# Fourteen projections of a decoder block as seven block products instead of eight, with GpSimd combining weights and VectorE summing blocks

## The chip, the cores and the metric

The program runs on one core of a Trainium2 chip. Its metric is the device time of one execution in microseconds. All of its data is f32. The core has TensorE (matmuls; PE in the profile, PEld its weight loads), VectorE (DVE), ScalarE (ACT), GpSimd (POOL) and SyncE (SP, which here only issues transfers). TensorE writes into eight banks of PSUM, of 128 partitions x 512 f32 each; the other operands are in SBUF.

## The reference, cut to what matters

The reference is one decoder layer on a sequence of 256 tokens of width 1024: a normalised input `h`, one wide projection of it split among a pooling mixer, an RWKV-7 mixer and a sparse attention (NSA), their merge, an output projection, and a mixture of experts.

```python
h = rms_norm(x, norm_mix)                     # 256 x 1024
t = h @ w_in                                  # all input projections at once
# columns: pooling 512 | r, k, v 3*512, loras 160 | q 1024, six K/V of 256, gates 48
pool_mixer: windows 2/4/8/16 over the sequence, pooled minus self, a map per group
rwkv7_mixer: u + (u_prev - u) * mu; decay, rates a, kk = k*k_k normalised; recurrent state
nsa_mixer: compressed keys kc, vc -> MLP; selected keys ks, vs; window keys kw, vw; 16 queries
x = x + merge(gated branches) @ w_out
x = x + hier_moe(rms_norm(x))
```

The change concerns 14 of the products `h @ w_in`, each with 256 of its columns.

## The kernel before, in words

All weights are repacked in chunks of 1 MB. A front chunk holds 256 columns of a 1024-deep matrix: 8 blocks `k` of 128 rows (on the partitions) by 256 columns. 48 front chunks pass through four slots of `ring` in the order of their numbers; SyncE loads chunk n once the chunk four before it has been given up (`taken`). Six steps of `ring` behind these four slots are not used for weights in the front: `bias`, `amat`, `qT` and `kT` lie there later. The 96 chunks of the experts follow, in the same way, in 23 slots all over SBUF.

`hT` is h transposed, 8 blocks of 128 channels by 256 tokens. A projection (`project`, L609 through `mm`) gives a chunk's 256 columns as two halves `m` of 128 rows, each the sum over 8 blocks `k` of a matmul with 128x128 weights and 256 tokens. That is 16 matmuls of 256 columns into one bank. In the order of the program `project` makes `pool1`, `rkv1` to `rkv6`, `kc`, `vc`, `q0` to `q3`, `ks` and `kw`. Other work stands in between: `wup` and `aup` (L698, L705: loras with 32 rows of weights), `kk0` and `kk1` (L714), the compression MLP (`mlp`, in two halves), `poolmix` (L729), `hidT`, `kcb`, `vcb`, `bonus` (L764), the scores `cs0` and `cs1` (L1007) and the transposes `tok` (L938).

ScalarE copies a bank that is full to SBUF (L1418) and frees it. VectorE then works on it: the pooling windows (`sums`), the mixing of each token with the one before it (`shift`: a subtract of 128x512 and two multiply-adds of 128x256 for each `rkv`), the squares for `kk`, the 16 scans of the decay (L1885), the windows of the compression, a reciprocal of 128x1024 (L1902) and a chain of twelve operations of 128x1024 to `rwkv_ready`. `raw` has two buffers, given back by `raw_used`. `tt`, `ts` and `stt` are VectorE's helpers, so that their lines (L1776, L1779, L1780, L1783) are those of many operations.

GpSimd clears three tiles, takes two roots for the normalisation (L1393), and has nothing more until 163 us (L1407, the masks of a triangular inverse, `lmask`).

The order of each engine is the order of the code. Every wait is on a semaphore; `bank_full` and `bank_free` of each bank count its uses in the order of `plan`. SyncE sends the relative bias through HBM (L546, L549) before it goes on with chunk 4.

## Time and profile before

| | us |
|---|---|
| median of 3 runs (lowest, highest) | 664.6 (664.16, 665.4) |
| the profiled execution | 663.38 |
| its span, first to last instruction | 661.6 |
| PE busy | 613.7 (93%) |
| DVE, ACT, POOL busy | 216.3, 141.3, 20.1 |

### The profile page before, as it was taken

The numbers are of one execution on the slowest core, as the hardware profiler recorded it, in microseconds if no ns is written. First come the engines' busy times: TensorE is split into PE (matmuls) and PEld (weight loads), VectorE is DVE, ScalarE is ACT, GpSimd is POOL, SyncE is SP. The second block draws the span as 40 slices with busy tenths as digits, with TensorE's granted clock in tenths as the row PEclk, the third lists the DMA queues.
The fourth block names the chain that finished last, engine by engine and source line by source line (L and its number), as shares of the span: only waits on it lengthen the run. The fifth ranks groups of instructions, "written<-read, shape, count | busy, mean of one in ns | idle before, by whom it ended". The sixth has DMA issues, their size and how long they took to land.

```text
span 661.6 us, 11832 instructions
## 1 busy us (share of the span) xinstructions
PE 613.7 (93%) x4992; PEld 450.1 (68%) x4992; DVE 216.3 (33%) x596; ACT 141.3 (21%) x356; POOL 20.1 (3%) x23
## 2 busy tenths in 40 slices
PE   8999999999999999999999999998999888858684
PEld 8988887888877777877778888886344433413241
DVE  3162548424333565345620122226111212012022
ACT  3010243132224263443531000001201111010013
POOL 1000000000200003000000000000000000000000
PEclk9999999989999999999999999999999999969698
DMA  8484335631211111011136996697999999999993
GB/s 326 185 314 181 127 128 190 259 124 65 85 46 65 66 64 65 12 55 66 64 115 276 423 419 229 255 423 274 398 421 419 421 421 420 420 423 421 421 394 129
DMA packets 27288, 158.96 MB, mean 240 GB/s; under 512 B 2896, under 2 KB 7136, under 8 KB 9440
## 3 DMA queue, kind: packets, MB, share of 16 engines
q1 hardware_dynamic: 24224, 137.71, 53.0%
q10 hardware_dynamic: 3008, 20.45, 7.4%
q8 instruction: 42, 0.69, 0.4%
q14 instruction: 14, 0.11, 0.0%
HBM read 157.07 MB, written 1.07 MB: 239 GB/s over the span
## 4 chain that ended last, share of the span: by engine, by line
PE 67%; issue 31%; ACT 1%; POOL 0%; DVE 0%; POOLq 0%; ACTq 0%; DVEq 0%
PE bank L609 45%; PE bank L840 5%; PE bank L938 3%; PE bank L641 2%; PE bank L967 2%; PE bank L987 2%; PE bank L624 1%; PE bank L997 1%; PE bank L951 1%; PE bank L1057 1%; PE bank L872 1%; PE bank L902 1%; PE bank L1007 1%; PE bank L891 1%; PE bank L1135 0%
## 5 line engine op out<-in xcount | busy, mean ns | idle before, releaser
L609 PE MATMUL bank<-hT,ring 128*128 128x256 f32 x864 | 199.9, 383 | 0.2 <-issue 0.2
L609 PEld LDWEIGHTS bank<-hT,ring 128*128 128x128 f32 x864 | 159.3, 190 | 31.4 <-issue 11.8
L609 PE MATMUL bank<-yT,ring 128*128 128x256 f32 x256 | 55.4, 379 | 0.0
L609 PEld LDWEIGHTS bank<-yT,ring 128*128 128x128 f32 x256 | 48.6, 190 | 6.6
L1418 ACT ACTIVATE work<-bank 128x512 f32<-128x512 f32 (+1 forms) x42 | 21.5, 511 | 110.9 <-PE bank L1239 48.9
L1776 DVE TENSOR_TENSOR work<-bank,table 128x512 f32<-128x512 f32 (+1 forms) x22 | 11.6, 544 | 94.1 <-PE bank L1232 85.5
L1285 PE MATMUL bank<-ring,work 128*32 128x512 f32 (+1 forms) x192 | 32.7, 615 | 10.4 <-DMA yT<-experts 7.2
L1232 PEld LDWEIGHTS bank<-work,tok 128*128 128x128 f32 x256 | 30.2, 192 | 10.0 <-issue 10.0
L1223 PE MATMUL bank<-ring,work 128*32 128x512 f32 x240 | 30.4, 612 | 2.6 <-DMA ring<-experts 2.6
L1232 PE MATMUL bank<-work,tok 128*128 128x128 f32 x256 | 31.5, 278 | 0.8 <-DVE work L1780 0.8
L1577 ACT ACTIVATE tok<-tok,small 128x128 f32<-128x128 f32 (+1 forms) x64 | 28.4, 445 | 14.5 <-DVE small L1995 12.6
L1293 PE MATMUL bank<-work 128*128 128x512 f32 (+1 forms) x68 | 29.9, 581 | 0.5 <-DVE work L2342 0.5
L609 PE MATMUL bank<-ring,work 128*128 128x256 f32 (+1 forms) x144 | 29.0, 358 | 0.0
L1783 DVE SCALAR_TENSOR_TENSOR work<-ring,bank 128x512 f32<-128x512 f32 x12 | 8.2, 687 | 58.7 <-PE bank L609 58.7
L609 PEld LDWEIGHTS bank<-ring,work 128*128 128x128 f32 x144 | 24.9, 190 | 2.8
L1293 PEld LDWEIGHTS bank<-work 128*128 128x128 f32 x68 | 12.2, 189 | 18.4 <-issue 17.3
L1783 DVE SCALAR_TENSOR_TENSOR work<-work,bank 128x256 f32<-128x256 f32 x8 | 3.4, 420 | 63.5 <-ACT work L1706 63.5
L1418 ACT ACTIVATE hT<-bank,table 128x128 f32<-128x128 f32 x12 | 3.6, 367 | 92.4 <-PE bank L1127 86.1
L1285 PEld LDWEIGHTS bank<-ring,work 128*32 128x32 f32 x192 | 8.6, 119 | 20.0 <-issue 17.9
L1995 DVE CUSTOM_DVE_ANT_0 tok<-bank,ring 128x128 f32<-128x128 f32 (+1 forms) x64 | 19.6, 352 | 7.5 <-PE bank L967 7.3
L1593 ACT ACTIVATE ring<-bank,small 128x256 f32<-128x256 f32 x24 | 10.1, 471 | 49.9 <-PE bank L609 49.9
L1418 ACT ACTIVATE t<-bank 128x512 f32<-128x512 f32 x16 | 9.6, 597 | 44.6 <-PE bank L840 26.6
(254 smaller groups left out, 748.3 us busy)
## 6 DMA issues: line engine op xcount, KB each, us to landing
ring<-front SPq DMA_DIRECT2D x47, 1024.0 KB, 4.9
ring<-experts SPq DMA_DIRECT2D x40, 1024.0 KB, 24.4
work<-experts SPq DMA_DIRECT2D x9, 1024.0 KB, 27.6
ring<-experts ACTq DMA_DIRECT2D x8, 1024.0 KB, 13.6
table<-experts SPq DMA_DIRECT2D x6, 1024.0 KB, 27.3
yT<-experts SPq DMA_DIRECT2D x6, 1024.0 KB, 26.8
hT<-experts SPq DMA_DIRECT2D x4, 1024.0 KB, 24.0
work<-experts ACTq DMA_DIRECT2D x3, 1024.0 KB, 27.8
```

The lines of the kernel that those rows point to most:

```text
L609: return first(pe.matmul(o, l, r, start=(k == 0), stop=(k == n - 1)))
L641: return first(pe.matmul(o[0:cols, col + i * P:col + (i + 1) * P], w[:, k, lo:lo + cols], hT[:, k, i * P:(i + 1) * P], start=(k == lo == i ...
L840: last = pe.matmul(o[rows, h * CH:(h + 1) * CH], left[rows, h, :], right[rows, h, :], start=True, stop=True)
L938: last = pe.transpose(o[:, b * P:(b + 1) * P], part, ident)
L967: last = pe.matmul(obank[p][:, hp * S:(hp + 1) * S], qT[rows, 2 * g + hp, i * P:(i + 1) * P], keys, start=True, stop=True)
L1223: last = pe.matmul(bank[4][CAP * e:CAP * (e + 1), :], gath[:, k, CAP * e:CAP * (e + 1)], w[:, e, :], start=(k == 0), stop=(k == KD - 1))
L1232: last = pe.matmul(o, tok[:, i, k * P:(k + 1) * P], sel[:, i, :], start=(i == 0), stop=(i == 1))
L1285: last = pe.matmul(o[CAP * e:CAP * (e + 1), 0:w], ghidT[:, f, CAP * e:CAP * (e + 1)], down[e][:, f, lo:lo + w], start=(f == 0), stop=(f == 1))
L1293: return pe.matmul(total[i][lo // 512][:, lo % 512:lo % 512 + w], wselT[:, i, :], ydown[:, lo:lo + w], start=False, stop=(gang == NGANG - ...
L1418: return act.activation(o, i_, ACT.Copy, scale=scale)
L1577: ins = act.activation(pb, pb, ACT.Exp, scale=-1.0, bias=astat[:, 8 * (n % 2) + b:8 * (n % 2) + b + 1], accum_out=astat[:, 16 + 8 * (n % 2 ...
L1995: ins = dve.tensor_tensor_reduce(prob[:, n % 2, bs], b0[:, bs], back, 1.0, FAR, ALU.add, ALU.min, astat[:, 8 * (n % 2) + b:8 * (n % 2) + b ...
```

## The change

A product of two 2x2 block matrices takes eight block products, or seven with 15 sums of blocks (Strassen's form as Winograd gave it). The weights of a chunk are split in four: the first and last four blocks `k`, and the two halves of the columns. `hT` is split by the same blocks `k` and by the two halves of the tokens. A block product (`quarter`) is 4 matmuls of 128 columns, so that a chunk has 28 of them in place of 16 of 256.

- The four sums of `hT` (`hdiff`) are made once, by VectorE.
- The four sums of the weights (`combo`, three buffers) are made by GpSimd for each of the 14 chunks, each 128x512.
- The sums of products: what can be summed by accumulation in the bank is left to TensorE. `first_half` makes four products in the four quarters of the bank; then VectorE's `sum_half` (a copy and three adds of 128x128) makes the value to which the rest is added; `second_half` makes three products, accumulated on what is there; then `sum_rest` (an add of 128x256) completes the bank and gives it to ScalarE.
- The first half of a chunk is issued ahead of the second half of the one before. The `rkv` chunks get three banks (4, 5, 7) in place of two, `q2` another bank.
- VectorE's pooling is cut in four and spread among the chunks, its reciprocal and its scans are cut, and ScalarE's root stands ahead of its copies of `vc`. Chunk 15 (`w1v`) and chunk 17 (`q2`) come earlier in the ring. SyncE's loop is unrolled, some semaphores are shared. `q1`, `pool0`, the loras and the three value chunks stay as they were.

```diff
+C_SPLIT = (C_POOL + 1,) + tuple(range(C_K, C_K + 6)) + (C_KC, C_VC, C_Q[0], C_Q[2], C_Q[3], C_KS, C_KW)
+FRONT = tuple(range(13)) + (13, 15, 17, 14, 16) + tuple(range(18, NFRONT))
+        hdiff = spare[:, 12288:14336].rearrange("p (j k t) -> p j k t", j=4, k=4)
+        combo = [spare[:, lo:lo + SLOT].rearrange("p (j k c) -> p j k c", j=4, k=4) for lo in (6144, 14336, 4096)]
+        partial = [vraw[:, P * n:P * (n + 1)] for n in range(3)]
+            def quarter(o, at, left, right, fresh=False):
+                for k in range(4):
+                    last = first(pe.matmul(o[:, at * P:(at + 1) * P], left[:, k, :], right[:, k, :],
+                                           start=(fresh and k == 0), stop=(k == 3), skip_group_check=True))
+                return last
+            def first_half(name, c):
...
+                quarter(o, 0, w[:, 0:4, 0, :], hT[:, 0:4, 0:P], fresh=True)
+                pe.wait_ge(q["combo_ready"], 4 * j + 1)
+                quarter(o, 1, g[:, 0, :, :], hdiff[:, 0, :, :])
+                pe.wait_ge(q["combo_ready"], 4 * j + 2)
+                quarter(o, 2, g[:, 2, :, :], hdiff[:, 2, :, :])
+                pe.wait_ge(q["combo_ready"], 4 * j + 3)
+                quarter(o, 3, g[:, 1, :, :], hdiff[:, 1, :, :]).then_inc(q["first_half"], 1)
+            def second_half(name, c):
...
+                pe.wait_ge(q["half_summed"], j + 1)
+                quarter(o, 0, w[:, 4:8, 0, :], hT[:, 4:8, 0:P])
+                quarter(o, 2, w[:, 4:8, 1, :], hdiff[:, 3, :, :])
+                pe.wait_ge(q["combo_ready"], 4 * j + 4)
+                quarter(o, 1, combo[j % 3][:, 3, :, :], hT[:, 4:8, P:2 * P]).then_inc(q["second_half"], 1)
+                pe_take()
@@ TensorE's order
-            project("pool1", C_POOL + 1)
+            first_half("pool1", C_POOL + 1)
             for c in range(1, 7):
-                project(f"rkv{c}", C_K + c - 1)
+                first_half(f"rkv{c}", C_K + c - 1)
+                if c == 1:
+                    second_half("pool1", C_POOL + 1)
+                else:
+                    second_half(f"rkv{c - 1}", C_K + c - 2)
@@ between wup and aup
+            second_half("rkv6", C_K + 5)
...
-            project("kc", C_KC)
-            project("vc", C_VC)
+            first_half("kc", C_KC)
+            first_half("vc", C_VC)
+            second_half("kc", C_KC)
...
+            first_half("q0", C_Q[0])
+            second_half("vc", C_VC)
+            second_half("q0", C_Q[0])
...
+            first_half("q3", C_Q[3])
+            first_half("ks", C_KS)
+            second_half("q3", C_Q[3])
@@ between cs0 and cs1, and behind tok
+                if i == 0:
+                    first_half("kw", C_KW)
-            project("kw", C_KW)
+            second_half("kw", C_KW)
@@ GpSimd
+            for j, c in enumerate(C_SPLIT):
...
+                pool.wait_ge(loaded[n % FRING], 16 * (n // FRING + 1))
+                if j >= 3:
+                    pool.wait_ge(q["second_half"], j - 2)
+                pool.tensor_tensor(g[:, 0, :, :], w01, w11, ALU.add).then_inc(q["combo_ready"], 1)
+                pool.tensor_tensor(g[:, 2, :, :], w00, w01, ALU.subtract).then_inc(q["combo_ready"], 1)
+                pool.wait_ge(q["combo_ready"], 4 * j + 1)
+                pool.tensor_tensor(g[:, 1, :, :], g[:, 0, :, :], w00, ALU.subtract).then_inc(q["combo_ready"], 1)
+                pool.wait_ge(q["combo_ready"], 4 * j + 3)
+                pool.tensor_tensor(g[:, 3, :, :], w10, g[:, 1, :, :], ALU.subtract).then_inc(q["combo_ready"], 1)
@@ VectorE
+            def sum_half(name, c):
...
+                dve.wait_ge(q["first_half"], j + 1)
+                chain(dve.tensor_copy(u, o[:, 3 * P:4 * P]))
+                chain(tt(u, u, o[:, 0:P], ALU.add))
+                chain(tt(v, u, o[:, P:2 * P], ALU.add))
+                chain(tt(o[:, 3 * P:4 * P], v, o[:, 2 * P:3 * P], ALU.add), "half_summed")
+            def sum_rest(name, c):
...
+                dve.wait_ge(q["second_half"], j + 1)
+                middle = bank[b][:, P:3 * P].rearrange("p (a t) -> p a t", a=2)
+                tt(middle, middle, like(partial[j % 2][:, None, :], [P, 2, P]), ALU.add).then_inc(bank_full[b], 1)
+            for c in range(2, 7):
+                sum_half(f"rkv{c}", C_K + c - 1)
+                sum_rest(f"rkv{c - 1}", C_K + c - 2)
+                if c < 5:
+                    pooled(c)
+                mixed(c - 1)
```

TensorE's order, before, at `rkv1` and `rkv2` (banks 5 and 4; slots 3 and 0):

```order
L609 MATMUL bank5<-hT,ring 128x256 [waits slot_loaded3]
L609 MATMUL bank5<-hT,ring 128x256 x15
L609 MATMUL bank4<-hT,ring 128x256 [waits bank_free4,slot_loaded0]
L609 MATMUL bank4<-hT,ring 128x256 x15
L609 MATMUL bank5<-hT,ring 128x256 [waits bank_free5,slot_loaded1]
```

The same place now: the first half of `rkv2` (bank 7) and the second half of `rkv1` (bank 5):

```order
L638 MATMUL bank7<-hT,ring 128x128 [waits slot_loaded0]
L638 MATMUL bank7<-hT,ring 128x128 x3
L638 MATMUL bank7<-ring 128x128 [waits combo_ready]
L638 MATMUL bank7<-ring 128x128 x3
L638 MATMUL bank7<-ring 128x128 [waits combo_ready]
L638 MATMUL bank7<-ring 128x128 x3
L638 MATMUL bank7<-ring 128x128 [waits combo_ready]
L638 MATMUL bank7<-ring 128x128 x3
L638 MATMUL bank5<-hT,ring 128x128 [waits half_summed]
L638 MATMUL bank5<-hT,ring 128x128 x3
L638 MATMUL bank5<-ring 128x128 x4
L638 MATMUL bank5<-hT,ring 128x128 [waits combo_ready]
```

A chunk that waited for its transfer and its bank alone now waits for GpSimd at four places and for VectorE at one.

VectorE's order before, from the end of the pooling on: the mixings follow each other, each behind ScalarE's copy (`raw_ready`).

```order
L1776 TENSOR_TENSOR yT<-t13 128x16 [waits dve_chain]
L1776 TENSOR_TENSOR work<-vraw 128x512 [waits raw_ready,pool_ready]
L1783 SCALAR_TENSOR_TENSOR work<-work,table,vraw 128x256 [waits dve_chain] x2
L1776 TENSOR_TENSOR work<-vraw 128x512 [waits dve_chain,raw_ready]
L1783 SCALAR_TENSOR_TENSOR work<-work,table,vraw 128x256 [waits dve_chain] x2
L1776 TENSOR_TENSOR work<-vraw 128x512 [waits dve_chain,raw_ready]
```

And now, from `sum_half` of `rkv4` (bank 5) on: `sum_rest` of `rkv3` (bank 4), the fourth part of the pooling, the mixing of `rkv3`, then `sum_half` of `rkv5` (bank 7).

```order
L1854 TENSOR_TENSOR vraw<-vraw,bank5 128x128 [waits dve_chain] x2
L1854 TENSOR_TENSOR bank5<-vraw,bank5 128x128 [waits dve_chain]
L1854 TENSOR_TENSOR bank4<-bank4,vraw 128x256 [waits second_half,half_summed]
L1964 COPY t13<-work 128x8 [waits bank_full4]
L1854 TENSOR_TENSOR t13<-work 128x248
L1861 SCALAR_TENSOR_TENSOR yT<-t13 128x256 [waits dve_chain]
L1854 TENSOR_TENSOR t13<-t13,table 128x16 [waits dve_chain]
L1854 TENSOR_TENSOR yT<-t13 128x16 [waits dve_chain]
L1854 TENSOR_TENSOR work<-vraw 128x512 [waits raw_ready,pool_ready]
L1861 SCALAR_TENSOR_TENSOR work<-work,table,vraw 128x256 [waits dve_chain] x2
L1911 COPY vraw<-bank7 128x128 [waits dve_chain,first_half]
```

What TensorE waits for (`half_summed`) is now queued behind pooling and mixing of earlier chunks. Of these, seven operations per chunk read two tensors in SBUF.

## Rows read from the trace of the kernel before

**Rows 1.** The page: busy time, share of the span, instructions of each engine.
```profile
PE 613.7 (93%) x4992; PEld 450.1 (68%) x4992; DVE 216.3 (33%) x596; ACT 141.3 (21%) x356; POOL 20.1 (3%) x23
```

**Rows 2.** Busy time by stretch: from:to, its length, then each engine.
```profile
core 0: us, PE busy (x) PEld busy (x) DVE busy (x) ACT busy (x) POOL busy (x), PEclk, DMA share, GB/s
26.00:155.00 129.00, 128.82 (x658) 109.31 (x662) 58.61 (x114) 29.49 (x52) 0.00 (x0) 0.99 0.49 180
77.50:137.70 60.20, 60.02 (x305) 49.65 (x304) 34.75 (x55) 16.90 (x26) 0.00 (x0) 1.00 0.52 193
380.00:661.00 281.00, 238.46 (x1547) 140.03 (x1546) 59.06 (x175) 28.59 (x70) 1.43 (x2) 0.95 0.92 372
```

**Rows 3.** Waits of TensorE up to 220 us: total, times, longest.
```profile
PE bank L624 <- POOL vraw L1385: 1.8, 1, 1.8
PE bank L641 <- ACTq L1430: 1.1, 1, 1.1
PE bank L609 <- issue: 0.2, 1, 0.2
```

**Rows 4.** The chain that ended last, 20 to 160 us: start, length, what.
```profile
19.97 4.99 PE bank L641 x45
...
25.96 48.80 PE bank L609 x224
...
77.64 14.01 PE bank L609 x64
...
141.04 3.56 PE bank L1007 x32
144.60 3.37 PE bank L938 x16
```

**Rows 5.** Transfers of the front: issues, TensorE's wait, time to landing after 50 us.
```profile
28.10 0.39 SPq L549 DMA_DIRECT2D ring<-bias_rows  x1
...
30.42 24.55 SPq L556 DMA_DIRECT2D ring<-front  x6
...
39.95 2.02 PEld L609 LDWEIGHTS bank<-hT,ring 128*128 128x128 f32 x10 [0.39 <-DMA ring<-front]
...
DMA to landing us min/median/max: 4.7/4.7/5.0
```

**Rows 6.** GpSimd's groups by shape: busy us, mean ns.
```profile
L1407 POOL TENSOR_TENSOR vraw<-ring,table 128x512 f32<-128x512 f32 x6 | 7.6, 1270 | 186.5 <-DVE ring L1776 168.7 <-PE bank L840 17.8
L1407 POOL TENSOR_TENSOR work<-ring,table 128x512 f32<-128x512 f32 x4 | 5.1, 1277 | 12.5 <-PE bank L840 12.5
```

**Rows 7.** Timeline, weight loads where the rows in use change: start, length, group.
```profile
77.57 13.68 PEld L609 LDWEIGHTS bank<-hT,ring 128*128 128x128 f32 x64 [0.33 <-issue]
```

**Rows 8.** Stretch (length, PE busy, granted clock, DMA); timeline of four transposes.
```profile
144.50:147.50 3.00, 3.00 (x16) 0.50 0.00 0
...
434.01 0.60 PE L1119 MATMUL bank<-table,tok 128*128 128x128 f32 x4
```

**Rows 9.** Timeline of VectorE: pooling, mixing, and a 128x128 operation from PSUM.
```profile
35.21 0.94 DVE L1776 TENSOR_TENSOR t<-work 128x762 f32<-128x762 f32 x1
...
37.50 0.43 DVE L1783 SCALAR_TENSOR_TENSOR yT<-work,t 128x256 f32<-128x256 f32 x1
37.96 0.17 DVE L1776 TENSOR_TENSOR work<-work,table 128x16 f32<-128x16 f32 x1
...
47.86 0.69 DVE L1776 TENSOR_TENSOR work<-vraw 128x512 f32<-128x512 f32 x1 [5.11 <-ACT vraw L1418]
48.59 1.01 DVE L1783 SCALAR_TENSOR_TENSOR work<-work,table,vraw 128x256 f32<-128x256 f32 x2
...
316.10 0.28 DVE L1995 CUSTOM_DVE_ANT_0 tok<-bank,ring 128x128 f32<-128x128 f32 x1
```

**Rows 10.** Timeline, 251.5 to 255.5 us: GpSimd and VectorE side by side.
```profile
252.25 1.27 POOL L1407 TENSOR_TENSOR vraw<-ring,table 128x512 f32<-128x512 f32 x1 [16.64 <-DVE ring L1776]
...
252.48 0.69 DVE L1776 TENSOR_TENSOR t<-bank,table 128x512 f32<-128x512 f32 x1 [0.30 <-PE bank L840]
...
253.48 1.27 POOL L1407 TENSOR_TENSOR work<-ring,table 128x512 f32<-128x512 f32 x1
253.54 1.23 DVE L1776 TENSOR_TENSOR small<-small,gate_t 128x2 f32<-128x2 f32 x1
```

**Rows 11.** Operations that use `gate_t`: duration ns min/median/max, shapes.
```profile
L1776 DVE TENSOR_TENSOR small<-small,gate_t x26: 160/162/1228, 149.9 to 338.5; 128x2 f32<-128x2 f32 x16, 128x4 f32<-128x4 f32 x8, 128x16 f32<-128x16 f32 x2
```

**Rows 12.** Timeline, 315 to 316.8 us.
```profile
315.13 1.65 POOL L1393 TENSOR_TENSOR small<-small,table 128x8 f32<-128x8 f32 x1 [43.17 <-DVE small L1779]
315.29 0.16 DVE L1776 TENSOR_TENSOR small<-small,gate_t 128x4 f32<-128x4 f32 x1
315.49 0.69 DVE L1776 TENSOR_TENSOR tok<-tok,small 128x512 f32<-128x512 f32 x1
```

More of the change, by code:

```diff
@@ L589, in end, with chunk @@
                 ins.then_inc(bank_full[plan[name][0]], 1)
-            def chunk(n):
+            def chunk(c):
+                n = FRONT.index(c)
                 pe.wait_ge(loaded[n % FRING], 16 * (n // FRING + 1))
@@ L1472, in _ @@
                     ins = act.activation(t1[:, c, :], b0[:, m * S:(m + 1) * S], ACT.Tanh, bias=halves[:, c:c + 1], scale=0.5)
-                give(ins, "decay_tanh", f"wup{n}")
+                give(ins, "rates_tanh", f"wup{n}")
             for n in range(2):
@@ L1479, in _ @@
                                          scale=0.5)
-                give(ins, "rate_tanh", f"aup{n}")
+                give(ins, "rates_tanh", f"aup{n}")
             for b, name in enumerate(("kc", "vc")):
+                if b:
+                    act.wait_ge(q["kk_max"], 2)
+                    act.activation(t3[:, :, :], t3[:, :, :], ACT.Sqrt).then_inc(q["kk_root"], 1)
                 b0 = full(act, name)
@@ L1515, in _ @@
             queries(1)
+            queries(2)
             b0 = full(act, "mlp")
@@ L1825, in _ @@
                 chain(ins, "halves_ready" if name == "b_merge" else None)
+            def sum_half(name, c):
+                j = C_SPLIT.index(c)
+                o = bank[plan[name][0]]
+                u, v = partial[j % 2], partial[2]
+                dve.wait_ge(q["first_half"], j + 1)
[4 more added lines that the diff above has]
+            def sum_rest(name, c):
+                j = C_SPLIT.index(c)
+                b, n = plan[name]
+                dve.wait_ge(q["second_half"], j + 1)
+                middle = bank[b][:, P:3 * P].rearrange("p (a t) -> p a t", a=2)
+                tt(middle, middle, like(partial[j % 2][:, None, :], [P, 2, P]), ALU.add).then_inc(bank_full[b], 1)
+                dve.wait_ge(bank_full[b], n + 1)
+            dve.wait_ge(q["hT_odd_ready"], 2)
+            near, far = hT[:, 0:4, :], hT[:, 4:8, :]
+            chain(tt(hdiff[:, 0, :, :], near[:, :, P:], near[:, :, 0:P], ALU.subtract))
+            chain(tt(hdiff[:, 2, :, :], far[:, :, P:], near[:, :, P:], ALU.subtract))
+            chain(tt(hdiff[:, 1, :, :], far[:, :, P:], hdiff[:, 0, :, :], ALU.subtract))
+            chain(tt(hdiff[:, 3, :, :], far[:, :, 0:P], hdiff[:, 1, :, :], ALU.subtract), "hdiff_ready")
             def shift(rows, c, j, tiles):
@@ L1869, in _, with decays, windows @@
                 dve.sem_inc(q["raw_used"], 1)
+            sum_half("pool1", C_POOL + 1)
+            sum_half("rkv1", C_K)
+            sum_rest("pool1", C_POOL + 1)
+            dve.wait_ge(q["u_ready"], 2)
+            pooled(1)
+            for c in range(2, 7):
[4 more added lines that the diff above has]
+                mixed(c - 1)
             dve.wait_ge(q["lora_g_tanh"], 1)
             chain(ts(mix[0:96, 13, :], mix[0:96, 13, :], 0.5, 0.5, ALU.mult, ALU.add), "lora_g_ready")
-            dve.wait_ge(q["win_ready"], 16)
+            dve.wait_ge(q["win_moved"], 32)
             for m in range(4):
                 chain(ts(bf[:, m, :], mix[:, m, :], pr("k_k")[:, m:m + 1], None, ALU.mult), hold=(m == 3))
+            sum_rest("rkv6", C_K + 5)
             chain(tt(t3[:, :, :], bf, bf, ALU.mult), "kk_sq_ready")
-            dve.wait_ge(q["decay_tanh"], 2)
+            mixed(6)
+            sum_half("kc", C_KC)
+            dve.wait_ge(q["rates_tanh"], 2)
             chain(ts(t1[:, :, :], t1[:, :, :], 1.0, -0.5 * DECAY, ALU.add, ALU.mult))
-            dve.wait_ge(q["rate_tanh"], 2)
-            for m in range(4):
-                for c in range(NCH):
-                    cs = slice(c * CH, (c + 1) * CH)
-                    chain(dve.tensor_tensor_scan(t2[:, m, cs], cn("ones")[:, 0:CH], t1[:, m, cs], 0.0, ALU.mult, ALU.add),
-                          hold=(m == 3 and c == 3))
-            for b, name in enumerate(("kc", "vc")):
+            dve.wait_ge(q["rates_tanh"], 4)
+            def decays(channels):
+                for m in channels:
+                    for c in range(NCH):
+                        cs = slice(c * CH, (c + 1) * CH)
+                        chain(dve.tensor_tensor_scan(t2[:, m, cs], cn("ones")[:, 0:CH], t1[:, m, cs], 0.0, ALU.mult, ALU.add),
+                              hold=(m == 3 and c == 3))
+            def windows(b):
                 dve.wait_ge(q["kshift_ready"], b + 1)
@@ L1900, in _ @@
                 dve.sem_inc(bank_free[plan[f"kk{n}"][0]], 1)
+            windows(0)
+            sum_half("q0", C_Q[0])
             dve.wait_ge(q["kk_root"], 1)
-            chain(dve.reciprocal(t3[:, :, :], t3[:, :, :]))
+            for m in range(4):
+                chain(dve.reciprocal(t3[:, m, :], t3[:, m, :]), hold=(m == 3))
+                if m == 0:
+                    sum_rest("vc", C_VC)
+                elif m == 2:
+                    sum_rest("q0", C_Q[0])
+            windows(1)
             chain(tt(bf, bf, t3[:, :, :], ALU.mult))
```

99 lines of the change are left out of this document (61 added, 38 removed).

## The prediction, made before the changed kernel ran

> **What bounds the kernel now.** I read the page's busy line first: TensorE 93% of the span, no other engine above a third [rows 1]. Then busy time by stretch: from 26 to 155 us, where the changed chunks lie, TensorE is busy all but 0.2 us of 129, VectorE 59, GpSimd not at all [rows 2]. Up to 220 us TensorE waits three times, 3.1 us in all [rows 3]. So the front is bound by the number and length of its matmuls. From 380 us on the queues share the bound (DMA share 0.92, TensorE busy 238 of 281 us [rows 2]). The transfers of that stage are released by what TensorE has consumed, so a front that ends x earlier or later moves the end by about x. Times below are of the profiled execution (663.4 us, span 661.6). The median of the three runs shown is 1.2 us above it, and I add 1.2 at the end. A difference under 0.2% (1.3 us) can't be told from none.
>
> **TensorE's side of the change.** Each f32 matmul leaves two records. Seven chunks take 224 records in 48.80 us, of which 0.39 is a wait for a transfer [rows 4, 5]: (48.80 - 0.39) / 7 = 6.92 us a chunk. A 128-column record costs 4.99 / 45 = 0.111 us [rows 4]; 28 matmuls are 56 records, 6.22 us. Gain 0.70 us a chunk, 9.8 for fourteen, a tenth and not the eighth by which the columns shrink. The waits between the quarters I put at nothing: the chain shows consecutive chunks without a gap although each begins with waits on a slot and a bank [rows 4].
>
> The first two chunks keep none of it. TensorE would have both first halves and the second half of `pool1` done at 25.9 + 0.2 + 44 x 0.222 = 35.9 us. The next chunk (`rkv2`) has its transfer issued at 30.42, behind the 2 MB table, and TensorE waited for it until 39.95 [rows 5]. Nothing in the change starts it earlier. And now GpSimd must first combine it: three operations of 1.27 us [rows 6] put the fourth quarter at 43.8, its end at 44.7, and after 12 more matmuls `rkv3` begins at 47.4. Before it began at 39.95 + 6.92 = 46.9, with nothing owed; now 12 matmuls (2.7 us) are. Behind by 3.2 us. The eleven chunks left give 7.7 back.
>
> Three smaller items. The rows at 74.7 to 77.6 hold 16 records of 256 columns in 2.89 us [rows 4], which laid end to end would be 16 x 0.216 = 3.5: `wup` and `aup` use different rows of the array and overlap. The second half of `rkv6` now stands between them, which costs 0.6 and two more changes of array shape (a third of a us of weight-load idling at such a place [rows 7], some 0.25 of it lost): 1.1. The chain's 16 transposes at 144.60 take 3.37 us, at a granted clock of 0.50, the 1.2 GHz level, where four at full clock take 0.60, tail of 0.28 included [rows 4, 8]: 16 x 0.11 = 1.8; what TensorE did before them was 16 matmuls of 14 or 30 columns (32 records [rows 4]). The first half of `kw` now splits these, and I expect the 2.4 GHz level to hold: 1.6 gained. Banks freed later (`kc` waits for ScalarE's `wup`, and `q3`, `ks` for VectorE) cost 1.2. Without anything else the front would end 7.7 - 3.2 - 1.1 + 1.6 - 1.2 = 3.8 us earlier.
>
> **GpSimd and VectorE.** GpSimd's four operations a chunk are 5.1 us, under the 6.22 of TensorE; transfers land 4.7 us after issue [rows 5] and a slot is refilled two periods ahead, so neither is the bound by itself. VectorE adds 4 operations of 128x128 and one of 128x256 a chunk. No row has that shape as an add; between 0.17 (128x16) and 0.42 (128x256) I take the 0.28 of another 128x128 operation [rows 9]: 4 x (0.28 + 0.04) + 0.46 = 1.8 us. Its own work is then at most 1.8 + 1.8 (pooling, 1.5 to 2.1) + 1.75 (mixing [rows 9]) = 5.3 us a chunk, again under 6.22. That sum supposes that the two engines don't disturb each other.
>
> The trace says that they do. At 253.48 GpSimd starts a 1.27 us operation that reads two tensors; at 253.54 VectorE starts a multiply of two columns by two columns, both inputs in SBUF, and it lasts 1.23 us, until GpSimd ends. Its 25 siblings have a median of 0.16 [rows 10, 11]. The VectorE operation at 252.48, during another GpSimd one, has one input in PSUM and keeps its 0.69. So a VectorE operation with two SBUF inputs is held for as long as GpSimd's large operation lasts. Before, GpSimd had ten of these; the change adds 56, back to back, in the stretch where VectorE's pooling, mixing and RWKV chain use two SBUF inputs.
>
> The Trainium skill, SBUF — State Buffer, section Who interferes with whom, has the same rule: the pair is held for a whole instruction, an operation with one SBUF input is free of it, and whoever comes second blocks; the trace agrees, with 1.23 for 0.16 us. It adds `tensor_scalar` and copies in their fast modes, which no row here shows; by that the 4 operations before `kk_sq` and the 4 of `kf` would be held as well, some 5 us more. The sum below leaves these at their own lengths.
>
> The price, by stage. (a) `rkv2` to `rkv4`: 7 two-input operations a chunk meet 4 of GpSimd; if three of the four hold one up in full, 5.3 + 3.8 = 9.1 against 6.2, 2.9 each, 8.7. `rkv5` and `rkv6` (mixing alone): 3.5 + 3.8 = 7.3, 1.1 each, 2.2. Together 10.9; ends 5 (one wait for each run of operations) and 15 (every GpSimd operation holds one up). TensorE pays because its second halves wait for VectorE's `half_summed`, which stands behind the mixing in VectorE's order. (b) Squares and mixing behind `rkv6`, which free the raw buffer, and with it ScalarE, bank 0 and `kc`: 3 (2 to 9). (c) From `kc` to `ks`: TensorE needs 60.2 - 6 x 0.70 - 3.6 = 52 us there; VectorE's own work is 34.8 [rows 2] + 6 x 1.8 = 45, so it has 7 to give. Six chunks' 24 operations (30 us) meet some 40 of VectorE; 14 in full are 18, less 7, 11 us (0 to 23), seen where `q3` and `ks` want their sums. In all 24.9 us, net 24.9 - 3.8 = 21.1 later: 663.4 + 21.1 + 1.2 = 686 us.
>
> **Rivals.**
> - No contention worth speaking of: VectorE's stretches are short and GpSimd yields. For it: at 315.13 a GpSimd power of 8 columns lasts 1.65 us and VectorE's two-input operations at 315.29 and 315.49 keep 0.16 and 0.69 [rows 12]. Against: that one reads 8 columns, the new ones 512, as at 253.48. Then the 3.8 us stand: 664.6 - 3.8 = 661 us. It decides as long as waits in all stay under 3.8 us beyond VectorE's idle time. This is the faster side.
> - Light contention: VectorE, once it has the port, keeps it through a run of chained operations, and GpSimd is the one that waits. One wait of 1.3 per run: (a) 5, (b) 2, (c) 2, less 3.8: 5 us later, 670 us.
> - Heavy: GpSimd's next operation follows its last without a gap (252.25, 253.48: 1.23 apart for 1.27 [rows 10]), so VectorE waits for two or three at a time. (a) 15, (b) 9, (c) 14 to 23, less 3.8: 35 to 43 later, about 702 us.
> - TensorE falling to 1.2 GHz in the new waits (one of 4.0 us at 35.9). Each such stretch like the one of [rows 8] costs up to 1.7 us; inside the others, with no time of its own.
>
> **How the numbers follow.** As forecast 0.60 (673 to 697), light 0.16, heavy 0.10, no contention 0.14. The likeliest is 686. Leaving out the faster case and the top of the heavy one gives 666 to 700. Faster 0.14; the light case within 0.2% now and then, 0.03; slower 0.83.
>
> **What would show it.** VectorE's two-input operations (128x512 subtract 0.69, 128x16 0.17 before) get means near or over 1 us, while the adds from PSUM stay at 0.3; GpSimd's 56 stay at 1.27 or are drawn out by VectorE's lengths. TensorE waits on VectorE with 5 us and more per chunk from `rkv3` on, and in front of the second half of `q3`. A wait of about 4 us for the transfer at 36 us. Full clock at the transposes behind `cs1`. I am wrong if the two-input operations keep their lengths; if they are long and TensorE has still no wait, VectorE had more room than I counted; if a chunk of 28 matmuls takes 6.9 us, the TensorE side fails.

## The result and the profile after

The changed kernel takes 690.67 us (median of 4 runs, 689.32 to 692.09), the kernel before 664.38 us (median of 4, 663.11 to 665.4). The ratio is 1.0397, with a 95% interval of 1.0365 to 1.0429: slower by 4%. The execution profiled took 692.09 us with a span of 690.3. All medians in this document are of fast executions; one slow execution, of the version with five split chunks (718.77 us at a granted clock of 0.842), is left out. Runs of the kernel before on other occasions lay between 660.1 and 669.0 us, so that one execution's span tells a difference of 2 us badly; a point inside the trace tells it well, and I use one below, the start of the first record of the stage behind `kw` (`L951` before, `L1011` after). It comes at 154.81 us before and at 180.77 after.

The page's busy line of the changed kernel, against [rows 1]: TensorE hardly more (617.4 us for 613.7), VectorE 60 us and GpSimd 82 us more.

```profile
PE 617.4 (89%) x5328; PEld 462.5 (67%) x5328; DVE 276.6 (40%) x673; ACT 141.3 (20%) x356; POOL 102.0 (15%) x79
```

Busy time by stretch of the changed kernel, the columns as in [rows 2]:

```profile
26.00:181.00 155.00, 130.21 (x989) 120.90 (x992) 110.90 (x179) 29.42 (x51) 76.15 (x52) 0.89 0.42 150
47.00:80.00 33.00, 28.10 (x224) 27.72 (x223) 27.11 (x46) 3.12 (x6) 24.85 (x19) 0.89 0.31 102
120.00:157.00 37.00, 27.08 (x209) 22.49 (x207) 32.98 (x34) 5.67 (x8) 25.76 (x16) 0.90 0.50 183
```

Before, the front held 129 us with TensorE idle for 0.2. Now it holds 155, TensorE is idle for 25 of them, and its granted clock is 0.89 instead of 0.99. From 120 to 157 it is VectorE that is busy nearly throughout (33 of 37). TensorE's own waits up to 220 us, against [rows 3]:

```profile
PE bank L638 <- DVE bank L1854: 13.9, 3, 9.0
PE bank L638 <- DMA ring<-front: 6.7, 1, 6.7
PE bank L638 <- ACTq L1507: 3.0, 1, 3.0
```

The same waits in TensorE's timeline (start, length of the group, the wait ahead of it in brackets; `L638` is a block product):

```profile
41.99 2.08 PE L638 MATMUL bank<-hT,ring 128*128 128x128 f32 x8 [6.73 <-DMA ring<-front]
43.86 4.42 PE L638 MATMUL bank<-ring 128*128 128x128 f32 x24
48.12 1.06 PE L638 MATMUL bank<-hT,ring 128*128 128x128 f32 x8
...
61.80 1.16 PE L638 MATMUL bank<-hT,ring 128*128 128x128 f32 x8 [1.01 <-DVE bank L1854]
...
65.47 2.84 PE L638 MATMUL bank<-ring 128*128 128x128 f32 x24
72.20 2.08 PE L638 MATMUL bank<-hT,ring 128*128 128x128 f32 x8 [3.89 <-DVE bank L1854]
...
78.58 2.84 PE L638 MATMUL bank<-ring 128*128 128x128 f32 x24
81.26 1.06 PE L638 MATMUL bank<-hT,ring 128*128 128x128 f32 x8
...
93.79 2.05 PE L638 MATMUL bank<-hT,ring 128*128 128x128 f32 x8 [2.98 <-ACTq L1507]
...
99.62 1.06 PE L638 MATMUL bank<-hT,ring 128*128 128x128 f32 x8
...
157.27 2.08 PE L638 MATMUL bank<-hT,ring 128*128 128x128 f32 x8 [9.03 <-DVE bank L1854]
...
162.55 0.63 PE L805 MATMUL bank<-table,xcmp 128*128 128x128 f32 x2
...
176.14 2.02 PE L998 MATMUL bank<-table,work 128*128 128x128 f32 x16
```

Two things are to be seen. One wait is for the transfer of `rkv2` (41.99); the others stand where the second half of a chunk wants VectorE's sum (61.80 for `rkv3`, 72.20 for `rkv4`, 157.27 for `q3`), and at `kc` (93.79). And behind each of the four longer ones eight records take 2.05 to 2.08 us instead of 1.06: TensorE has fallen to the 1.2 GHz level. What that costs can be read from the starts. Behind the wait at 61.80, at full clock, 32 records take 3.67 us (to 65.47); behind those at 41.99, 72.20 and 93.79 they take 6.13, 6.38 and 5.83 (granted clock 0.58, 0.56 and 0.60), and the 24 behind 157.27 take 5.28 for 2.78 (0.50). That is 2.5, 2.7, 2.2 and 2.5 us, 9.9 in all, beside the waits themselves. The last row is the group of transposes (16 records) behind `cs1`, 3.55 us long before and 2.02 now, at full clock.

VectorE's groups by shape from 26 to 175 us (busy, mean ns of one). First the changed kernel, then the same lines of a kernel that is the changed one without GpSimd's sums (the first experiment):

```profile
L1861 DVE SCALAR_TENSOR_TENSOR work<-work,table,vraw 128x256 f32<-128x256 f32 x12 | 14.7, 1226 | 0.4
L1854 DVE TENSOR_TENSOR work<-vraw 128x512 f32<-128x512 f32 x6 | 6.1, 1020 | 1.7 <-ACT vraw L1495 1.6
...
L1857 DVE TENSOR_SCALAR work<-work,table 128x256 f32<-128x256 f32 x4 | 5.1, 1343 | 0.0
...
L1911 DVE COPY vraw<-bank 128x128 f32<-128x128 f32 x14 | 4.1, 292 | 20.9 <-PE bank L638 20.1
```
```profile
L1857 DVE SCALAR_TENSOR_TENSOR work<-work,table,vraw 128x256 f32<-128x256 f32 x12 | 5.8, 485 | 0.4
L1850 DVE TENSOR_TENSOR work<-vraw 128x512 f32<-128x512 f32 x6 | 4.2, 692 | 1.7 <-ACT vraw L1491 1.6
L1854 DVE TENSOR_SCALAR work<-work,table 128x256 f32<-128x256 f32 x4 | 1.1, 349 | 0.0
L1907 DVE COPY vraw<-bank 128x128 f32<-128x128 f32 x14 | 4.1, 291 | 25.3 <-PE bank L638 24.6
```

What reads SBUF twice takes 1.2 us instead of 0.49; what reads PSUM (the last row of each) keeps its length. The 9 us in front of the second half of `q3` begin here, in the changed kernel's timeline:

```profile
136.71 1.81 DVE L1854 TENSOR_TENSOR work<-work 128x1024 f32<-128x1024 f32 x1
...
137.40 2.26 POOL L1470 TENSOR_TENSOR ring<-ring 128x512 f32<-128x512 f32 x1
138.56 5.14 DVE L1857 TENSOR_SCALAR work<-work,table 128x256 f32<-128x256 f32 x4
...
139.62 1.32 POOL L1472 TENSOR_TENSOR ring<-ring 128x512 f32<-128x512 f32 x1
...
141.01 1.27 POOL L1474 TENSOR_TENSOR ring<-ring 128x512 f32<-128x512 f32 x1
142.24 1.32 POOL L1469 TENSOR_TENSOR ring<-ring 128x512 f32<-128x512 f32 x1
```

Four operations of 0.35 us take 5.14 us: they get one turn for each of GpSimd's operations. Behind them stand, in VectorE's order, four more of 128x256 (5.58 us at 145.94), and only then the sums that the second halves of `q3` and `ks` wait for.

### The profile page after: what moved, and what is told of

The parts are those of the page before. It is cut to its first block, busy times and chain, and to the rows that moved or that the text cites. A ratio compares the mean times of both kernels' runs of the same rounds, so it can differ in the third digit from the quotient of the medians.

```text
span 690.3 us, 12528 instructions
## 1 busy us (share of the span) xinstructions
PE 617.4 (89%) x5328; PEld 462.5 (67%) x5328; DVE 276.6 (40%) x673; ACT 141.3 (20%) x356; POOL 102.0 (15%) x79
## 4 chain that ended last, share of the span: by engine, by line
PE 56%; issue 30%; DVE 9%; DMA 2%; ACT 1%; SPq 0%; POOL 0%; POOLq 0%; DVEq 0%; ACTq 0%
PE bank L623 28%; PE bank L638 9%; PE bank L900 5%; DVE work L1861 3%; PE bank L998 2%; DVE work L1854 2%; PE bank L1027 2%; PE bank L1047 2%; PE bank L690 2%; DMA ring<-front 1%; DVE work L1857 1%; PE bank L673 1%; PE bank L1011 1%; PE bank L1057 1%; PE bank L1119 1%
## 5 line engine op out<-in xcount | busy, mean ns | idle before, releaser
L623 PE MATMUL bank<-hT,ring 128*128 128x256 f32 x416 | 101.8, 386 | 0.0
L623 PEld LDWEIGHTS bank<-hT,ring 128*128 128x128 f32 x416 | 74.5, 190 | 17.7 <-issue 9.8
L638 PE MATMUL bank<-hT,ring 128*128 128x128 f32 x336 | 50.2, 301 | 23.6 <-DVE bank L1854 13.9
L638 PEld LDWEIGHTS bank<-hT,ring 128*128 128x128 f32 x336 | 46.0, 213 | 27.1 <-DVE bank L1854 14.5
L638 PE MATMUL bank<-ring 128*128 128x128 f32 x448 | 59.8, 290 | 1.2 <-POOL ring L1472 1.0
L638 PEld LDWEIGHTS bank<-ring 128*128 128x128 f32 x448 | 57.2, 206 | 1.7 <-POOL ring L1472 1.2
L1347 PE MATMUL bank<-ring,work 128*32 128x512 f32 (+1 forms) x192 | 36.4, 678 | 10.2 <-DMA yT<-experts 7.2
L1455 POOL TENSOR_TENSOR small<-small,table 128x1 f32<-128x1 f32 (+2 forms) x5 | 5.2, 1031 | 234.8 <-DVE small L1861 136.6
L1469 POOL TENSOR_TENSOR ring<-ring 128x512 f32<-128x512 f32 x14 | 19.1, 1366 | 60.9 <-DMA ring<-front 52.5
## 6 DMA issues: line engine op xcount, KB each, us to landing
work<-experts SPq DMA_DIRECT2D x9, 1024.0 KB, 27.7
```

The source lines that it names most:

```text
L623: return first(pe.matmul(o, l, r, start=(k == 0), stop=(k == n - 1)))
L638: last = first(pe.matmul(o[:, at * P:(at + 1) * P], left[:, k, :], right[:, k, :], start=(fresh and k == 0), stop=(k == 3), skip_group_che ...
L1347: last = pe.matmul(o[CAP * e:CAP * (e + 1), 0:w], ghidT[:, f, CAP * e:CAP * (e + 1)], down[e][:, f, lo:lo + w], start=(f == 0), stop=(f == 1))
L1469: pool.tensor_tensor(g[:, 0, :, :], w01, w11, ALU.add).then_inc(q["combo_ready"], 1)
```

## The experiments

All times below are medians against runs of the kernel before made with them (663.5 to 664.3 us). "Front" is the point named above, before 154.81, after 180.77.

**1. Without GpSimd's sums.**

```diff
-                pool.tensor_tensor(g[:, 0, :, :], w01, w11, ALU.add).then_inc(q["combo_ready"], 1)
-                ... (the other three)
+                for _ in range(4):
+                    pool.sem_inc(q["combo_ready"], 1)
-                quarter(o, 1, g[:, 0, :, :], hdiff[:, 0, :, :])
+                quarter(o, 1, w[:, 0:4, 1, :], hdiff[:, 0, :, :])
```

> The changed kernel with GpSimd's 56 weight sums left out (it only counts its semaphore up when the chunk has landed, and the three quarters that used the sums read blocks of the chunk itself, so that every matmul, every VectorE addition and every order stays; the projections come out as other numbers). Theory: what the change costs is VectorE's operations being held by GpSimd's. Then VectorE's 128x256 operations from SBUF return from 1.2-1.4 us to 0.35-0.5 us, the 9.0 us wait in front of the second half of q3 goes, and the time is about 661 us (657 to 666), below the 664.4 of before. Rival 1, lateness of the sums: GpSimd's five-and-more us per chunk delay the quarters; the time falls as well, but VectorE's lengths are then no matter. Rival 2, cost on TensorE and VectorE of the split itself (28 matmuls that wait for four adds each): the time stays above 680 us with the waits for VectorE in place.

Measured: 664.06 us, ratio 1.0001 (0.9977 to 1.0026), front 153.10. The waits of TensorE that are left:

```profile
PE bank L638 <- DMA ring<-front: 3.9, 1, 3.9
...
PE bank L638 <- DVE bank L1850: 0.8, 2, 0.6
...
PE bank L638 <- ACTq L1503: 0.5, 1, 0.5
```

The sums cost 26.6 us, all of the loss; the split itself costs nothing that these runs resolve, but doesn't gain either. VectorE's busy time over the whole kernel falls from 276.6 to 241.6 us, so that the holding took 35 us of it. The front is 1.7 us earlier, not 3.8.

**2. Sums replaced by operations as long that read little.**

```diff
-                pool.tensor_tensor(g[:, 0, :, :], w01, w11, ALU.add).then_inc(q["combo_ready"], 1)
-                ... (the other three)
+                ...
+                for p in (0, 2, 1, 3):
+                    pool.tensor_tensor(g[:, p, 0, 0:6], cn("ones")[:, 0:6], cn("neghalf")[:, 0:6], ALU.pow)\
+                        .then_inc(q["combo_ready"], 1)
```

> The changed kernel with each of GpSimd's 56 sums replaced by a GpSimd power of 6 columns on constants (410 + 155 a column from its 1, 2 and 8 column rows, so about 1.3 us each, as long as a sum), at the same place and with the same signal; the quarters read blocks of the chunk itself, so the projections come out as other numbers. It keeps the lateness of the sums and takes their traffic away. Theory, VectorE held by operations that read whole blocks: VectorE keeps its lengths of the run without sums (128x256 scalar_tensor_tensor 0.49, tensor_scalar 0.35) and the time is 664 to 668 (the third chunk's last quarters come some 2 us later). Rival, lateness of the sums: what the sums cost stays, 685 to 691 us.

Measured: 663.99 us, ratio 1.0005 (0.9983 to 1.0027), front 153.25. GpSimd's group, and two of VectorE's:

```profile
L1472 POOL TENSOR_TENSOR ring<-table 128x6 f32<-128x6 f32 x56 | 76.1, 1387 | 50.7 <-DMA ring<-front 49.4 <-PE bank L638 1.4
```
```profile
L1860 DVE SCALAR_TENSOR_TENSOR work<-work,table,vraw 128x256 f32<-128x256 f32 x12 | 5.8, 485 | 0.4
...
L1856 DVE TENSOR_SCALAR work<-work,table 128x256 f32<-128x256 f32 x4 | 1.1, 349 | 0.0
```

GpSimd is nearly as busy as with the sums (76 us against 82, 1.39 us each against a mean of 1.49), TensorE waits as before for each of its signals, and the time is that of the run without them. So the lateness of the sums is worth nothing that can be told; it is something that the sums do and the powers don't. The difference meant is the reading and writing of whole blocks. That the powers are also another operation than an add is not separated by this run.

**3. GpSimd's sums added to the kernel before, nobody waiting.**

```diff
+            for j, n in enumerate((2, 3, 4, 5, 6, 7, 8, 9, 10, 11, 15, 18, 19, 20)):
+                pool.wait_ge(loaded[n % FRING], 16 * (n // FRING + 1))
+                ...
+                for p in range(4):
+                    pool.tensor_tensor(idle[j % 2][:, p, :], par[:, 0:512], par[:, 512:1024], ALU.add)...
```

> The kernel before with 56 GpSimd additions of 128x512 added, four each time that one of fourteen front chunks lands, on constants into unused memory; nobody waits for them. Nothing else is changed. Theory: VectorE's operations with SBUF inputs are held all the same: 128x256 scalar_tensor_tensor from 0.49 to about 1.2 us, tensor_scalar from 0.35 to about 1.3, adds with an input in PSUM and scans at their lengths. VectorE was busy 59 of 129 us there and has room for part of it: 2 to 8 us later than 664.4, so 666 to 672. Rival 1 (only the lateness of the sums costs): no change of the time and none of VectorE's lengths. Rival 2 (the split costs): no change either.

Measured: 666.77 us, ratio 1.0041 (1.0014 to 1.0068), front 158.57. VectorE is held as in the changed kernel:

```profile
L1792 DVE SCALAR_TENSOR_TENSOR work<-work,table,vraw 128x256 f32<-128x256 f32 x12 | 14.7, 1225 | 0.4
```

Over the whole kernel VectorE is busy 22.7 us longer (239.0 for 216.3). The two groups of four `tensor_scalar` operations of 128x256 were met less than expected, with means of 0.35 and 0.57 us and not 1.3. Yet the front is only 3.8 us later, and not by a wait for VectorE. TensorE's one new wait is for a transfer (2.7 us). The timeline of VectorE, then that of the transfer queue of this kernel, shows why:

```profile
21.65 1.52 DVE L1785 TENSOR_TENSOR work<-vraw 64x256 f32<-64x256 f32 x1 [7.76 <-ACT vraw L1427]
23.21 1.38 DVE L1792 SCALAR_TENSOR_TENSOR work<-work,table,vraw 64x256 f32<-64x256 f32 x1
24.62 1.37 DVE L1785 TENSOR_TENSOR work<-vraw 96x256 f32<-96x256 f32 x1
26.03 1.37 DVE L1792 SCALAR_TENSOR_TENSOR work<-work,table,vraw 96x256 f32<-96x256 f32 x1
...
28.05 0.55 DVE L1853 COPY work<-bank 16x384 f32<-16x384 f32 x1
```
```profile
28.63 0.34 SPq L546 DMA_DIRECT2D bias_rows<-work  x1
30.16 0.39 SPq L549 DMA_DIRECT2D ring<-bias_rows  x1
...
33.80 9.86 SPq L556 DMA_DIRECT2D ring<-front  x4
```

Four mixing operations are held to 1.4 us each, the copy of the bias row comes 2 us later, with it the 2 MB table, and behind the table on the same queue the chunk `rkv2` (issued at 33.80 against 30.42 [rows 5]). TensorE starts it 2.1 us later and loses 1.7 more at a lower clock behind that wait (0.92 from 26 to 47 us). Where TensorE has no wait for VectorE in each chunk, a held VectorE costs it nothing here except through what is queued behind VectorE.

**4. Each sum in two operations of half the size.**

```diff
-                pool.tensor_tensor(g[:, 0, :, :], w01, w11, ALU.add).then_inc(q["combo_ready"], 1)
+                pool.tensor_tensor(g[:, 0, 0:2, :], w01[:, 0:2, :], w11[:, 0:2, :], ALU.add)
+                pool.tensor_tensor(g[:, 0, 2:4, :], w01[:, 2:4, :], w11[:, 2:4, :], ALU.add).then_inc(...)
```

> The changed kernel with each of GpSimd's 56 sums cut into two operations of 128x256 (112 in all, 0.65 to 0.7 us each, so 5.2 to 5.6 us a chunk). Theory, an operation of VectorE is held until the GpSimd operation in flight ends: the held operations last at most one GpSimd operation of 0.7 us, 128x256 ones about 0.7 to 0.8 instead of 1.23, and the time falls by 5 to 12 us from 690.7, to about 682. Were VectorE held for as long as GpSimd's whole queue runs, or if the two shared the port in small steps, the lengths and the time would not change (688 to 692). Rival, lateness of the sums: they get later by GpSimd's issue of twice as many operations, so the time rises by 0 to 3 us.

Measured: 677.87 us, ratio 1.0209 (1.0165 to 1.0252); 12.8 us faster than the changed kernel, with more work for GpSimd. The held operations shrink with the holder:

```profile
L1865 DVE SCALAR_TENSOR_TENSOR work<-work,table,vraw 128x256 f32<-128x256 f32 x12 | 10.0, 832 | 0.4
...
L1861 DVE TENSOR_SCALAR work<-work,table 128x256 f32<-128x256 f32 x4 | 2.9, 784 | 0.0
```

So the hold lasts for one instruction of GpSimd, not for its queue. The `vraw` subtract of 128x512 went the other way, from 1.02 to 1.16 us mean: in the changed kernel two of its six are held (1.71 and 1.64 us, the others 0.69), with half-size sums all six (1.10 to 1.19). Why all six are met then stays open.

**5. `rkv2` and `rkv3` loaded ahead of the table.** With the sums, and without them:

```diff
+            for n in (4, 5):
+                sp.wait_ge(taken, n + 1 - FRING)
+                sp.dma_start(ring[:, (n - 4) * SLOT:(n - 3) * SLOT], front[FRONT[n]]).then_inc(loaded[n - 4], 16)
             sp.wait_ge(q["win_row"], 1)
```

> The changed kernel with the loads of the chunks rkv2 and rkv3 issued ahead of the 2 MB table. TensorE's wait of 6.7 us at 36 and the half clock behind it go. Theory: behind it TensorE is paced by VectorE, whose held operations run from chunk to chunk; so a part comes back as longer waits for VectorE: 3 to 6 us earlier than 690.7, 686. Rival, the transfer is the pace setter of the stage: all of it, 7 to 8 us, 683. Rival, nothing (the wait is only moved): 690.

> The changed kernel without GpSimd's 56 weight sums (the quarters read blocks of the chunk itself, other numbers come out) and with the loads of rkv2 and rkv3 issued ahead of the 2 MB table: what the split would bring if its sums were free and no chunk late. Theory: 3.9 us of wait and 1.2 us of half clock behind it go, 4 to 5 us earlier than the run without sums alone (664), so 659 to 660. Rival, the time is set by the expert transfers behind 380 us: no change against 664.

Measured with sums: 678.69 us, ratio 1.0215 (1.0179 to 1.025), front 171.51. Without: 657.04 us, 0.9902 (0.9868 to 0.9935), front 147.65. Both gains are larger than I expected, 12.0 and 7.0 us. Without sums the front comes 5.45 us earlier, near what was expected; the other 1.6 lies behind it. With sums the front comes 9.3 us earlier, and `wup` 11.9: the late transfer had not been hidden behind VectorE's delay, it came on top of it. In the changed kernel VectorE itself stood idle for 9.7 us before its sum at 48.39, waiting for the products of the late chunk. Later 2.6 us are lost again: the wait at `kc` for ScalarE is 5.7 instead of 3.0.

**6. Sums for the first seven chunks only.**

```diff
+                if j >= 7:
+                    ...
+                    for _ in range(4):
+                        pool.sem_inc(q["combo_ready"], 1)
+                    continue
```

> The changed kernel with GpSimd's sums made for the first seven chunks only (pool1 to rkv6); for the last seven (kc, vc, q0, q2, q3, ks, kw) GpSimd only signals and the quarters read blocks of the chunk itself (other numbers come out). By the traces with and without sums, TensorE reaches kc 14.4 us later with them and loses another 13.3 between kc and the small scores. If these are separate, this kernel keeps the first and saves the second: 677 to 678. If the delay of the first stage gives VectorE and TensorE room in the second, which swallows part, more is saved: under 672; if the second delay is a consequence of the first, it stays: 685 to 690.

Measured: 675.44 us, ratio 1.0163 (1.0117 to 1.021), front 164.67. The later seven are worth 15 to 16 us, the first seven 11.4. That is 2 us less than separate stages were to give (677 to 678). The difference is the wait at `kc`, 0.5 us here and 3.0 in the changed kernel, which I had put down to the first seven. It belongs to the sums of `kc` and `vc`, which run at the same time: in the changed kernel VectorE's mixing at 86.17 and a `tensor_scalar` at 89.11, ahead of the sum that ScalarE waits for, take 2.78 and 1.11 us for 1.01 and 0.29 here. But for that the two stages are separate.

**7. `kw` in two plain halves, in the kernel before.**

The transposes took 3.37 us in the chain of before, at a granted clock of 0.50 [rows 4, 8]. At full clock they were to take 1.8, so that the time falls by 1.6 us (0.5 to 2.5), to 662.8.

```diff
+            def kw_half(m):
+                ...
+                if i == 0:
+                    kw_half(0)
...
-            project("kw", C_KW)
+            kw_half(1)
```

> The kernel before, with the projection kw in two plain halves of 8 matmuls of 256 columns each: the first between the two small score products cs0 and cs1, the second behind the transposes that follow cs1. The same matmuls, no block products, nothing on GpSimd. [...] Rival: the low clock has another cause (the wait on VectorE ahead of it) or is only moved: no change, 664.4 +- 0.7.

Measured: 663.05 us, ratio 0.999 (0.9967 to 1.0012), which is no difference that can be told. The trace shows one in the group that is to answer for it:

```profile
147.68 2.02 PE L938 MATMUL bank<-table,work 128*128 128x128 f32 x16
```

This was 3.55 us before; the granted clock is 1.00 here, and the front comes at 153.09, 1.7 us earlier. The mechanism is there, and its 0.25% is smaller than what these runs resolve.

**8. Versions that might beat both.** The two orders alone (plain halves of `kw`, early loads); with them three chunks as block products, `pool1`, `rkv1` and `kw`; and five, with `rkv4` and `rkv5`:

```diff
+C_SPLIT = (C_POOL + 1, C_K, C_KW)
+C_SPLIT = (C_POOL + 1, C_K, C_K + 3, C_K + 4, C_KW)
```

> The kernel before with the two orders alone: kw in two plain halves around the second small score product, and the loads of rkv2 and rkv3 ahead of the 2 MB table. No block products, nothing on GpSimd. If the gain of the version with three split chunks (2.9 us) comes from the block products, this one has 2.0 us less of it than that: 1.6 for the clock and 0.4 for the transfer, 662.3. If the orders alone are the gain, 661.4 as there.

> The changed kernel with only three chunks as seven block products (pool1, rkv1, kw, where VectorE has little to do), the other eleven whole, the loads of rkv2 and rkv3 ahead of the 2 MB table. GpSimd makes 12 sums in place of 56. Theory: 3 x 0.7 for the products, 1.6 for the full clock at the transposes, 0.4 for the transfer, less about 1.5 for VectorE's lora mixing held by the first 8 sums and for the order of the second half of rkv1: 2 to 3 us earlier than 663.8 of before, 661. Rival (the split costs wherever it stands): 664 to 667.

> The version with three split chunks, with two more, rkv4 and rkv5 (20 GpSimd sums). If VectorE's room of some 3.4 us in each whole chunk's time on either side swallows what the 8 sums hold up (4 to 8 us), the two products give 1.4 us more: 660.0 against 661.4. If a held addition makes TensorE wait in front of the second halves, 662 to 664.

| version | us | ratio (95%) | front |
|---|---|---|---|
| orders alone | 662.28 | 0.9975 (0.9952 to 0.9997) | 152.64 |
| three split | 661.36 | 0.9962 (0.9947 to 0.9977) | 150.80 |
| five split | 661.03 | 0.9941 (0.9915 to 0.9967) | 151.50 |

Three chunks put the front 1.8 us ahead of the orders alone, near the 2.0 expected of three products; two more, which were to bring it 1.4 earlier, put it 0.7 later. VectorE is busy 25 of the 33 us from 47 on with five, 14 with three, and the granted clock there is 0.95 instead of 1.00. By the runs five and three are not told apart. By the front, under 2 us is left of the block products on this kernel.

## Why the prediction was right, step by step

The change was forecast at 686 us and measured 690.7. What holds VectorE up, and that TensorE pays for it behind `half_summed`, was forecast rightly. That the number came so near is in part luck: the holding was priced too high, and TensorE's clock was left at nothing. Most of the steps can be read against the runs with and without sums. The table has the time (us) at which TensorE reaches a place:

| | `rkv2` | `wup` | `kc` | `cs0` | front |
|---|---|---|---|---|---|
| before | 39.95 | 74.68 | 77.58 | 140.88 | 154.81 |
| no sums | 39.25 | 72.09 | 79.42 | 141.40 | 153.10 |
| after | 41.99 | 84.03 | 93.79 | 169.07 | 180.77 |
| sums for seven | 41.48 | 83.65 | 90.98 | 152.97 | 164.67 |
| after, early load | | 72.11 | 84.55 | 159.81 | 171.51 |
| no sums, early load | | 66.64 | 73.97 | 135.95 | 147.65 |

- **A chunk at 6.22 us.** Right: a quarter starts 0.892 us behind the last, seven are 6.24.
- **The first two chunks keep none of their gain.** Without sums the numbers are right, but not the reason: a transfer wait of 3.9 us where 4.0 was forecast, and `rkv3` begun at 46.98 for 47.4. The forecast came to 47.4 by three operations of GpSimd behind the landing. That run has none; in their place it has 1.4 us at the lower clock (granted 0.71 from 39.2 to 44.3 us). With the powers, as long as sums, `rkv3` begins at 48.76. With the sums the wait is 6.7 us. "Nothing in the change starts it earlier", I wrote, and didn't ask what starts it later: VectorE's held mixing, the bias row, the table, all ahead of it.
- **The three small items.** `wup` and `aup` with the half chunk between them: 6.8 us from `wup` to the wait at `kc` without sums, less 2.7 for the half, against 2.9: 1.2 lost, 1.1 forecast. Banks freed late: 0.5 and 0.8, 1.3 against 1.2. The transposes: 2.02 us for 3.55, 1.5 against 1.6.
- **Net without contention, 3.8 us.** Wrong by 2.1: the front of the run without sums is 1.7 us earlier, and its time 664.06 and not 661. The step that failed is the rival on TensorE's clock that I gave "no time of its own". The wait of 0.54 us at `kc` was followed by a stretch at the lower level (granted 0.68) even without sums; these are that kernel's rows there, and below them the same place with the powers of experiment 2:

```profile
79.42 1.77 PE L638 MATMUL bank<-hT,ring 128*128 128x128 f32 x8 [0.54 <-ACTq L1503]
80.98 3.87 PE L638 MATMUL bank<-ring 128*128 128x128 f32 x24
```
```profile
81.20 1.13 PE L638 MATMUL bank<-hT,ring 128*128 128x128 f32 x8 [0.55 <-ACTq L1506]
```

At full clock the first two are 1.06 and 2.84, 1.7 us less. With the powers the same wait had no such price, and in the changed kernel the waits of 1.0 us at 61.80 and at 147.08 had none. So a short wait may or may not be followed by the lower clock; the four of 3 us and more in the changed kernel all were, for 9.9 us against 3.1 without sums. That is a term of the sum, and it was left out.
- **Contention, stage (a): 10.9 us.** Measured 11.9 at `wup` (84.03 against 72.09), but not made of what it was said to be. 2.7 us are the later transfer, 4.9 the waits for VectorE at `rkv3` and `rkv4`, 3.8 more are lost at the lower clock behind these waits than without sums, and 0.5 are in small pieces. With the early load the same difference is 5.5 (72.11 against 66.64), near the lower bound given. The size was right by luck. Laid beside the run without sums, operation by operation, the 20 sums of `rkv2` to `rkv6` hold up 12 operations of VectorE, by 10.2 us in all: none for `rkv2`, one for `rkv3`, and 11 for the other three. The sum had 15 of 20 at 1.27 us each. It also added GpSimd's full length to the held operation's own, while a held operation of 0.49 lasts 1.37 in all, 0.89 more.
- **Stage (b): 3 us.** Measured 2.4 at `kc` (14.4 less 11.9), as forecast for bank 0; by experiment 6 this belongs to the sums of `kc` and `vc`, which run at that time.
- **Stage (c): 11 us.** Measured 13.3 (75.28 from `kc` to `cs0` against 61.98), and the same 13.3 with the early load. Up to the end of the wait for `q3`'s sum it is 11.3 (63.48 against 52.15 from `kc` on), as forecast; the other 2.0 come behind it, from the stretch at the lower clock. The 11.3 are again not made as said. VectorE is held up 17 times, by 15.2 us in all, for 14 times and 18 us forecast, and it had 3.9 us to give and not 7. Of the 15.2 us 4.0 are those of the four `tensor_scalar` of `kf`, 4 x (1343 - 349) ns, which the sum left at their own length because no row of before showed it. The page "SBUF — State Buffer" of the Trainium skill, section Who interferes with whom, had named it, and this case's trace now agrees. Of the other four named with them, in front of `kk_sq`, no hold is seen (mean 348 ns): GpSimd had no work then.
- **Sum of contention: 24.9 us.** Measured 27.7 at the front (180.77 less 153.10), 26.6 in the medians. By cause: TensorE's waits are 24.7 us against 5.2 without sums, 19.5 more; the lower clock takes 9.9 against 3.1, 6.8 more; 1.4 are in small pieces. The forecast had 24.9 for the waits and nothing for the clock. So two errors, of some 5 and 7 us, went opposite ways. Net 21.1 was forecast, against 26.0 at the front and 26.3 in the medians.
- **A front that ends x later moves the end by about x.** Right for the large numbers: 26.0 at the front, 26.3 in the medians.
- **The signs.** VectorE's two-input operations near or over 1 us, the adds from PSUM at 0.3, GpSimd's operations drawn out, a wait in front of `q3`'s second half and full clock at the transposes all came. Waits for VectorE of 5 us and more per chunk from `rkv3` on did not: they are 1.0 and 3.9 at `rkv3` and `rkv4`, and none at `rkv5` and `rkv6`.
- **Rivals.** No contention is excluded by experiments 1 and 2: its 661 us were the price without sums, and nearly that. The light case (GpSimd waits, VectorE keeps the port) is excluded by the four operations at 138.56, which got one turn each. The heavy one (VectorE waits for two or three at a time) is too: the longest 128x256 operations last 1.4 us. GpSimd is drawn out as well, but by less: means of 1.37 to 1.61 us for 1.27.

## What to carry to other kernels

Before work is given to an idle engine, look at what it shares with the busy ones: 56 operations of GpSimd that nobody waited for cost 3 us here, and 27 where each chunk's second half waits for a sum of VectorE's. Count, at each VectorE operation that reads SBUF twice or a `tensor_scalar`, one GpSimd operation instead of its own length, follow what stands behind VectorE into the transfer queues, and make GpSimd's operations small where the two must overlap. And a wait of TensorE is to be priced with the stretch at the lower clock that may stand behind it: 2.2 to 2.7 us for each of the four long waits here, 1.4 and 1.7 for two in the run without sums, nothing for those of 1.0 us.

## What the runs showed of the hardware beyond that

- A GpSimd power of 6 columns lasts 1.39 us and holds nothing that shows: VectorE's 128x256 two-input operations kept 485 ns beside 56 of them, as [rows 12] showed for one. So it isn't how long a GpSimd operation lasts that counts. That it is how much it reads and writes fits all runs, but a large power or a small add was not tried.
- The hold is mutual and by instruction. Where VectorE's held operation is itself long (1.8 us for 128x1024 at 136.71), GpSimd's next one lasts 2.26 us for 1.27; half-size GpSimd operations cut a held `tensor_scalar` from 1.34 to 0.78 us.
- Small copies in SBUF are held as well: two of 128x6 and 128x8 took 610 and 473 ns in the changed kernel, 169 and 170 without the sums.
- What stays open: why all six `vraw` subtracts are held with half-size sums and two with whole ones; what decides whether a short wait of TensorE is followed by the lower clock; and where the 1.6 and 2.7 us came from that the early loads gave behind the front; single executions differ there by as much.
